# High weights times both token halves in one product of 512 columns, in the mixers and the first fills

## Chip, cores and metric
One core of one Trainium2 chip runs the whole program in one launch. The metric is the time on the device in microseconds, as the median of several executions. TensorE (PE) multiplies, ScalarE (ACT) and VectorE (DVE) copy, split and add, GpSimd (POOL) and the DMA queues of SyncE (SP) bring data.

## What is computed
The reference runs 256 tokens of width 1024 in float32 through two blocks. The first block:

```python
h = rmsnorm(x, norm1_g); proj = h @ w_in
(x_rnn, g_rnn, dq, dk, dv, fq, fk, fv, f_logit, gates) = split(proj)
y_rnn = gelu(g_rnn) * rg_lru(causal_dwconv(x_rnn))
y_diff = rmsnorm(diff_attention(dq, dk, dv))        # 4 heads
y_fox = forgetting_attention(fq, fk, fv, log_f)     # 8 heads
g = sigmoid(gates + gate_b)
x = x + (g[0]*(y_rnn @ w_br_rnn) + g[1]*(y_diff @ w_br_diff) + g[2]*(y_fox @ w_br_fox)) @ w_out
x = x + (gelu(u_gate) * u_val) @ ffn_down           # u = conv(rmsnorm(x) @ ffn_up)
```

The second block has two layers. Each layer is a mixer and an expert stage:

```python
qa, ka, va, qw, kw, vw, gates = split(rmsnorm(h) @ w_in)
oa = dilated_mixture(qa, ka, va); ob = banded_attention(qw, kw, vw)
h = h + (g[0] * (oa @ w_branch_a) + g[1] * (ob @ w_branch_b)) @ w_out
h = h + expert_choice_ffn(rmsnorm(h))               # 16 experts, each on 32 tokens
```

## The kernel before
**Split products.** All dense products but those of the experts are made from split numbers. The normed tokens lie transposed as a high and a low half (`HT.h`, `HT.l`, eight tiles of 128 x 256 each). Weights come in slabs of 128 x 4096 (2 MB) and each slab is cut into four pieces of 128 x 1024. ScalarE copies a piece rounded to its high part (`high`, L1906) and VectorE subtracts this from the piece to get the low part (`low`, L1227). TensorE then adds three products for each tile (`mm3`, L590 to L592): high weights times high tokens, high weights times low tokens, low weights times high tokens. The fourth is left out.

**Pieces and banks.** In the form used for keys, queries and gates (`piece`, with the views `PAIRS`) a piece holds four of the eight row blocks for 256 output columns. Two pieces fill one bank of 128 x 512, with the 128 columns of one group in its left half and those of the next in its right half. So two pieces are 48 products of 256 columns, and ScalarE copies the finished bank out once (`QF`, `KF`, `QW`, `KW`, `QA`, `KA`), or applies tanh with a bias twice (`GT`, `GL`, the gates).

**Buffers for split pieces.** `buffer_plan` gives each piece a buffer and says at which piece of the list the next ones are split (`split_at`). In the first fills (pieces `fq`, `fk` and `gates`, 32 of them) and in the fills of each layer there are three buffers: `split(t)` splits piece t+2, whose buffer was that of piece t-1. In the query and key stage of a layer (`qka`) there are six buffers and `split(t)` splits piece t+5.

**Order of work.** Each engine runs one list in order. Where attention is computed, the order is made by `schedule`: one step is `ffstfwv` in the first fills and `swftfv` in a layer. f is one fill, that is a piece of a later product; s computes scores on TensorE, takes row maxima on VectorE and exponentials on ScalarE; w scales by the row sums on VectorE; t turns tiles on TensorE and copies them on ScalarE or VectorE; v multiplies by the values on TensorE, and ScalarE and VectorE take the output apart into high and low. A step handles s of one unit and w, t and v of the three units before. The first fills have 8 units (4 of one attention, 4 of the other) and 32 fills, the layers 12 units (4 and 8) and 28 fills, two of which are token products of their own kind that the change doesn't touch (`tok_fill`). PE takes `sched_f` and `sched_l` without w; ACT without w and with s as exponentials (`first_exp` L2099, `layer_exp` L2198); DVE with row maxima (L1472).

**Names.** `first_fill` and `layer_fill` exist in the lists of TensorE and ScalarE. `bank_f` and `bank_l` give the bank of each fill. `sides`, `side`, `block`, `query_bank` and `filled` come with the change.

## Time and profile before

| | us |
|---|---|
| median of 3 runs | 1816.87 (1815.5 to 1817.04) |
| the profiled execution, whole | 1819.09 |
| its span, first to last instruction | 1817.3 |
| TensorE busy | 1528.7 (84%) |
| VectorE busy | 762.0 (42%) |
| ScalarE busy | 596.6 (33%) |
| data moved by DMA | 567.44 MB, 312 GB/s on average |

The first block ends near 495 us. The mixer of the first layer runs from there to about 725 us and its experts to 1150 us; the second layer's mixer to about 1385 us and its experts to the end. Busy time tells how much an engine did, the chain of waits what the end waited for, and the timeline in what order an engine took its work. The idle time in brackets in a timeline row stands before that row's first instruction, with the instruction that ended it.

### The profile page before, as it was taken

What the parts mean: (1) busy time and instruction counts of PE and PEld (TensorE: products, weight loads), DVE (VectorE), ACT (ScalarE), POOL (GpSimd) and SP (SyncE); (2) the same over time, 40 slices, a digit from 0 to 9 for tenths busy, and PEclk for the clock granted to TensorE, in tenths of its full rate; (3) what the DMA queues carried; (4) which work ended last, traced back from release to release, by engine and by line L of the source; (5) the groups of instructions that cost most, each with busy time, mean ns of one, the idle gap of its engine ahead of it and who ended that gap; (6) DMA issues with size and microseconds to landing.
All of it is one profiled execution on the core that took longest, in us unless ns stands there. A gap on an engine that the chain in (4) does not pass through costs nothing.

```text
span 1817.3 us, 34044 instructions
## 1 busy us (share of the span) xinstructions
PE 1528.7 (84%) x15288; PEld 1178.5 (65%) x15288; DVE 762.0 (42%) x1574; ACT 596.6 (33%) x1063; POOL 76.0 (4%) x87
## 2 busy tenths in 40 slices
PE   8999999999999999976666656999999966666665
PEld 8989998999799998532333322799896523232332
DVE  6896668887565656210101110546664201011011
ACT  5765546665455654000000000546642000000001
POOL 1020001000020101000000000001010000000000
PEclk9999999999999999997888898999999988888888
DMA  6543446555473568999999999853589999999997
GB/s 263 186 143 140 165 172 235 189 184 200 163 282 120 206 259 352 421 429 430 431 430 429 431 429 430 359 190 129 212 325 412 428 430 430 430 430 429 430 430 310
DMA packets 45841, 567.44 MB, mean 312 GB/s; under 512 B 6672, under 2 KB 7216, under 8 KB 10496
## 3 DMA queue, kind: packets, MB, share of 16 engines
q1 hardware_dynamic: 40176, 552.62, 74.2%
q0 software_dynamic: 3744, 12.03, 1.9%
q8 instruction: 120, 1.97, 0.4%
q10 hardware_dynamic: 1776, 0.62, 0.2%
q14 instruction: 25, 0.20, 0.0%
HBM read 564.18 MB, written 1.05 MB: 311 GB/s over the span
## 4 chain that ended last, share of the span: by engine, by line
PE 60%; DMA 33%; DVE 3%; another core or an unknown queue 2%; ACT 1%; issue 0%; SPq 0%; DVEq 0%; ACTq 0%
DMA slab<-in_slabs 32%; PE bank L590 14%; PE bank L591 14%; PE bank L592 14%; PE bank L1135 6%; PE bank L1187 3%; PE bank L1205 1%; PE bank L947 1%; PE bank L1006 1%; PE bank L970 1%; DMA sm<-in_fb 1%; DVE wl L1227 1%; PE bank L1112 1%; DVE xc L1350 0%
## 5 line engine op out<-in xcount | busy, mean ns | idle before, releaser
L1135 PE MATMUL bank<-slab,xe 128*32 128x256 f32 x4096 | 302.4, 449 | 166.6 <-DMA slab<-in_slabs 166.5
L1227 DVE TENSOR_TENSOR wl<-slab,wh 128x1024 fp32r<-128x1024 f32 (+1 forms) x286 | 348.1, 1231 | 186.4 <-ACT wh L1906 186.1
L590 PE MATMUL bank<-hth,wh 128*128 128x256 f32 x1344 | 387.3, 288 | 1.8 <-DVE wl L1227 1.7
L591 PE MATMUL bank<-htl,wh 128*128 128x256 f32 x1344 | 380.0, 283 | 0.0
L592 PE MATMUL bank<-hth,wl 128*128 128x256 f32 x1344 | 379.9, 283 | 0.0
L1906 ACT ACTIVATE wh<-slab 128x1024 fp32r<-128x1024 f32 (+1 forms) x286 | 296.2, 1046 | 168.9 <-PE bank L592 157.8
L1135 PEld LDWEIGHTS bank<-slab,xe 128*32 128x32 f32 x4096 | 139.5, 125 | 310.1 <-DMA slab<-in_slabs 207.8
L590 PEld LDWEIGHTS bank<-hth,wh 128*128 128x128 f32 x1344 | 257.3, 191 | 11.9 <-issue 7.8
L591 PEld LDWEIGHTS bank<-htl,wh 128*128 128x128 f32 x1344 | 257.5, 192 | 0.1
L592 PEld LDWEIGHTS bank<-hth,wl 128*128 128x128 f32 x1344 | 257.3, 191 | 0.0
L1187 PE MATMUL bank<-slab,ha 128*32 128x256 f32 x2048 | 140.1, 421 | 78.7 <-DMA slab<-in_slabs 77.7
L2302 ACT ACTIVATE ta<-bank 128x256 f32<-128x256 f32 x32 | 12.3, 384 | 516.4 <-PE bank L1135 516.4
L1187 PEld LDWEIGHTS bank<-slab,ha 128*32 128x32 f32 x2048 | 70.6, 118 | 134.0 <-DMA slab<-in_slabs 93.9
L1862 DVE SCALAR_TENSOR_TENSOR ta<-ta,bank 128x256 f32<-128x256 f32 x32 | 13.5, 422 | 287.3 <-ACT ta L2302 287.3
L2308 ACT ACTIVATE ha<-bank 128x256 f32<-128x256 f32 x32 | 12.3, 384 | 273.6 <-PE bank L1170 273.6
L1867 DVE SCALAR_TENSOR_TENSOR ta<-bank,ta 128x256 f32<-128x256 f32 x32 | 13.6, 425 | 209.1 <-PE bank L1135 209.1
L1874 DVE COPY ye<-bank 128x256 f32<-128x256 f32 x32 | 13.6, 425 | 207.9 <-PE bank L1187 207.9
L1205 PE MATMUL bank<-ye,gz 32*128 32x256 f32 x512 | 49.0, 454 | 18.5 <-DVE ye L1874 15.7
L2198 ACT ACTIVATE sx<-sx,sm 128x256 f32<-128x256 f32 (+1 forms) x80 | 41.5, 520 | 60.0 <-DVE sm L1715 43.7
L2386 POOL DMA_DIRECT2D bias<-in_bias x40 | 22.1, 556 | 844.8 <-PE bank L1205 421.1
L1205 PEld LDWEIGHTS bank<-ye,gz 32*128 32x128 f32 x512 | 21.6, 198 | 52.1 <-DVE ye L1874 33.6
L1645 DVE SCALAR_TENSOR_TENSOR u<-bank,pv,u 128x255 f32<-128x255 f32 x88 | 40.4, 480 | 16.5 <-ACT u L2172 14.9
(388 smaller groups left out, 2181.7 us busy)
## 6 DMA issues: line engine op xcount, KB each, us to landing
slab<-in_slabs SPq DMA_DIRECT2D x251, 2048.0 KB, 47.8
slab<-in_slabs SPq DMA_DIRECT2D x23, 1024.0 KB, 10.3
bias<-in_bias POOLq DMA_DIRECT2D x32, 192.0 KB, 3.1
bias<-in_bias POOLq DMA_DIRECT2D x8, 256.0 KB, 5.9
x<-in_x SPq DMA_DIRECT2D x2, 512.0 KB, 4.5
rg<-in_rg POOLq DMA_DIRECT2D x1, 1024.0 KB, 10.4
bt<-in_rel POOLq DMA_DIRECT2D x1, 768.0 KB, 14.6
fg<-in_final_g POOLq DMA_DIRECT2D x1, 512.0 KB, 3.6
```

The source lines that it names most:

```text
L590: e.matmul(o, wh, xh, start=start, stop=False, skip_group_check=True)
L591: e.matmul(o, wh, xl, start=False, stop=False, skip_group_check=True)
L592: return e.matmul(o, wl, xh, start=False, stop=stop, skip_group_check=True)
L947: t = e.matmul(bk[d][:, qb * 256:(qb + 1) * 256], QW[hd, c, qb * 128:(qb + 1) * 128], KW[hd, c // 4, :], start=True, stop=True)
L1135: t = e.matmul(bk[bank][32 * j:32 * j + 32, 0:256], XE[:, c, :], w[:, k, 256 * j:256 * j + 256], start=(c == 0), stop=(c == 7))
L1187: t = e.matmul(bk[3][32 * j:32 * j + 32, 0:256], HA[:, o_:o_ + 32], w[:, k, 256 * j:256 * j + 256], start=(kk == 0), stop=(kk == 7))
L1205: t = e.matmul(bk[b][:, (j % 2) * 256:(j % 2) * 256 + 256], GZ[rows_, tb * 128:(tb + 1) * 128], YE[rows_, :], start=False, stop=(ex == 15) ...
L1227: e.tensor_tensor(lo, src, hi.bitcast(F32), ALU.subtract).then_inc(*dve_l.mark(p))
L1645: t = e.scalar_tensor_tensor(o[:, d:256], ps[:, 0:256 - d], par("fw", (2 - d) * 44 + m), o[:, d:256], ALU.mult, ALU.add)
L1906: e.activation(hi, src, ACT.Copy).then_inc(*act_h.mark(p))
L2198: t = e.activation(S_[:, q * w:(q + 1) * w], S_[:, q * w:(q + 1) * w], ACT.Exp, bias=c_nm[:, st + q:st + q + 1], accum_out=c_dn[:, st + q: ...
L2386: e.dma_start(btiles[n % 4][:, 0:w], I["bias"][n, :, 0:w]).then_inc(*s_bt[n % 4].mark((l, n), 16))
```

## The change
Where it applies, a piece now holds all eight row blocks for 128 output columns (`v_block`, `BLOCKS`). `HT`'s high and low halves are seen as one tile (`HT.both`), so that one product of 512 columns multiplies the high weights by both; the low weights times the high tokens go into the left half of the bank in a second product of 256 columns. The bank then holds two sides of the same 128 x 256 result. ScalarE copies the right side out to the destination (`side`), VectorE adds the left side to it (`sides`), and for gates ScalarE applies tanh to the destination in place, after the add. It applies to all 32 first fills, to 10 of the 12 pieces of each layer's query and key stage, and to 26 of the 28 fills of each layer. The fills alternate between banks 3 and 7. Who waits for `fk`, `qka` or `fill` before scores now waits for VectorE's add.

```diff
+def v_block(c):
+    return lambda ap: ap.rearrange("p (k n) -> p k n", k=8)[:, :, 128 * c:128 * c + 128]
+BLOCKS = [v_block(c) for c in range(4)]
-    add("fq", 0, PAIRS)
-    add("fk", 0, PAIRS)
+    add("fq", 0, BLOCKS)
+    add("fk", 0, BLOCKS)
...
+                self.both = row(name + "b", hi, 2 * n * cols, F32R).rearrange("p (s n c) -> p s n c", s=2, n=n)
+                self.h, self.l = self.both[:, 0, :, :], self.both[:, 1, :, :]
...
+    bank_f, bank_l = {k: 3 if k % 2 else 7 for k in range(32)}, fill_banks(sched_l, 0, 0)
+    bank_l.update({k: 3 if k % 2 else 7 for k in range(4, 28)})
+    bank_l.update({0: 6, 1: 7, 2: 3, 3: 6})
...
+        def block(p, b, X2):
+            wh, wl = halves(p, 8, 128)
+            bank_free(b)
+            for k in range(8):
+                e.matmul(two(bk[b][:, :]), wh[:, k, :], X2.both[:, :, k, :], start=(k == 0), stop=False, skip_group_check=True)
+                t = e.matmul(bk[b][:, 0:256], wl[:, k, :], X2.h[:, k, :], start=False, stop=(k == 7), skip_group_check=True)
+            t.then_inc(*pe_w.mark(p))
...
         def first_fill(k):
             p, b = fills_f[k][0], bank_f[k]
-            piece(p, b, k % 2, 2, 4, HT)
-            if k % 2:
-                reader[b] = [(act_s, ("fk", k // 2 - 2) if 4 <= k < 8 else ("fill", "f", k))]
+            block(p, b, HT)
+            reader[b] = [(dve_s, ("fa", "f", k))]
...
+        def sides(o, b, step):
+            V.wait_ge(*act_s["side", step])
+            e.tensor_tensor(o, o, bk[b][:, 0:256], ALU.add).then_inc(*dve_s.mark(step))
...
         for kind, i in sched_f:
             if kind == "f":
+                V.wait_ge(*pe_w[fills_f[i][0]])
+                dst = QF[:, i, :] if i < 4 else KF[:, i - 4, :] if i < 8 else GT[:, i - 8, :]
+                sides(dst, bank_f[i], ("fa", "f", i))
                 split(fills_f[i][0])
...
+                if 2 <= i < 12:
+                    V.wait_ge(*pe_w[p])
+                    sides((QA if i < 6 else KA)[:, i % 6, :], query_bank(l, i), ("qka", l, i))
                 split(p)
...
-                    for p in fills_l(l)[i]:
+                    ps = fills_l(l)[i]
+                    if len(ps) == 1:
+                        V.wait_ge(*pe_w[ps[0]])
+                        sides(filled(i), bank_l[i], ("fa", l, i))
+                    for p in ps:
                         split(p)
...
+        def side(o, p, b, step):
+            A.wait_ge(*pe_w[p])
+            e.activation(o, bk[b][:, 256:512], ACT.Copy).then_inc(*act_s.mark(("side", step)))
...
         def first_fill(k):
+            dst = QF[:, k, :] if k < 4 else KF[:, k - 4, :] if k < 8 else GT[:, k - 8, :]
+            side(dst, fills_f[k][0], bank_f[k], ("fa", "f", k))
             split(fills_f[k][0])
...
+            n = k - 8
+            if n >= 0:
                 A.wait_ge(*dve_s["hb"])
...
+                A.wait_ge(*dve_s["fa", "f", k])
+                e.activation(GT[:, n, :], GT[:, n, :], ACT.Tanh, bias=c_hb[:, 16 + n:17 + n],
+                             scale=0.5).then_inc(*act_s.mark(("fill", "f", k)))
...
             ps, b = fills_l(l)[k], bank_l[k]
+            if len(ps) == 1:
+                side(filled(k), ps[0], b, ("fa", l, k))
             for p in ps:
                 split(p)
...
+            n = k - 12
+            if n >= 0:
+                A.wait_ge(*dve_s["fa", l, k])
+                e.activation(GL[:, n, :], GL[:, n, :], ACT.Tanh, bias=c_hg[:, 16 * l + n:16 * l + n + 1],
+                             scale=0.5).then_inc(*act_s.mark(("fill", l, k)))
```

## Rows read from the trace of the kernel before

**Rows 1.** The page, chain that ended last, shares of the span
```profile
PE 60%; DMA 33%; DVE 3%; another core or an unknown queue 2%; ACT 1%; issue 0%; SPq 0%; DVEq 0%; ACTq 0%
```

**Rows 2.** Windows: busy us (instructions) of each engine, granted clock, DMA share, GB/s
```profile
630.00:640.00 10.00, 10.00 (x83) 8.95 (x82) 6.89 (x20) 7.24 (x19) 0.00 (x0) 1.00 0.00 0
700.00:710.00 10.00, 10.00 (x46) 8.29 (x45) 5.56 (x6) 3.94 (x4) 0.00 (x0) 1.00 1.01 430
```

**Rows 3.** Timeline of TensorE (start, us, instruction): ends of two unbroken runs
```profile
95.83 0.39 PE L591 MATMUL bank<-wl,hth 128*128 128x512 f32 x1
...
103.99 0.39 PE L591 MATMUL bank<-wl,hth 128*128 128x512 f32 x1
...
153.51 0.28 PE L590 MATMUL bank<-hth,wh 128*128 128x256 f32 x1
...
155.90 0.28 PE L592 MATMUL bank<-hth,wl 128*128 128x256 f32 x1
```

**Rows 4.** Timeline of two steps of the first fills
```profile
148.94 0.28 PE L590 MATMUL bank<-hth,wh 128*128 128x256 f32 x1
...
149.14 0.84 ACT L2128 ACTIVATE gt<-bank,sm 128x256 f32<-128x256 f32 x2 [1.02 <-PE bank L592]
...
152.88 0.29 DVE L1472 CUSTOM_DVE_ANT_0 sd<-bank,bt 128x128 f32<-128x128 f32 x1 [0.60 <-PE bank L796]
...
154.32 0.40 ACT L2099 ACTIVATE sd<-sd,sm 128x128 f32<-128x128 f32 x1 [3.39 <-DVE sm L1541]
...
156.09 1.04 ACT L1906 ACTIVATE wh<-slab 128x1024 fp32r<-128x1024 f32 x1
...
157.17 1.23 DVE L1227 TENSOR_TENSOR wl<-slab,wh 128x1024 fp32r<-128x1024 f32 x1 [2.42 <-ACT wh L1906]
157.75 0.36 ACT L2107 ACTIVATE o<-bank 128x256 f32<-128x256 f32 x1
158.02 1.05 ACT L1906 ACTIVATE wh<-slab 128x1024 fp32r<-128x1024 f32 x1
158.31 0.17 DVE L1547 RECIPROCAL sm<-sm 128x4 f32<-128x4 f32 x1
```

**Rows 5.** Layer 0, one step: chain (TensorE's scores), then timeline of VectorE and ScalarE
```profile
623.44 1.06 PE bank L947 x8
...
632.32 1.06 PE bank L947 x8
...
624.55 0.42 DVE L1472 CUSTOM_DVE_ANT_0 sx<-bank,bias 128x256 f32<-128x256 f32 x1 [0.22 <-PE bank L947]
...
626.44 0.51 ACT L2198 ACTIVATE sx<-sx,sm 128x256 f32<-128x256 f32 x1 [2.58 <-DVE sm L1715]
...
628.52 1.04 ACT L1906 ACTIVATE wh<-slab 128x1024 fp32r<-128x1024 f32 x1
629.47 1.05 ACT L2209 ACTIVATE ptl<-bank 128x512 f32<-128x512 f32 x2
630.43 1.04 ACT L1906 ACTIVATE wh<-slab 128x1024 fp32r<-128x1024 f32 x1
631.38 0.81 ACT L2234 ACTIVATE gl<-bank,sm 128x256 f32<-128x256 f32 x2
...
632.79 0.42 DVE L1745 TENSOR_TENSOR obl<-bank,obh 128x256 fp32r<-128x256 f32 x1
```

**Rows 6.** Chain in order of time: scores of steps 0, 5 and 7, first fills
```profile
122.60 0.86 PE bank L796 x8
...
173.90 1.51 PE bank L811 x16
...
196.79 1.53 PE bank L811 x16
```

**Rows 7.** Timeline of TensorE behind a wait
```profile
34.29 0.39 PE L590 MATMUL bank<-hth,wh 128*128 128x256 f32 x1 [1.67 <-DVE wl L1227]
34.52 0.28 PE L591 MATMUL bank<-htl,wh 128*128 128x256 f32 x1
```

More of the change, by code:

```diff
@@ L163, in piece_list @@
     add("fv", 0, TOKS)
-    add("fq", 0, PAIRS)
-    add("fk", 0, PAIRS)
+    add("fq", 0, BLOCKS)
+    add("fk", 0, BLOCKS)
     for i in range(6):
-        add("gates", i, PAIRS)
+        add("gates", i, BLOCKS)
     for i in range(2):
@@ L180, in piece_list @@
         for i in range(3):
-            add(f"qka{l}", i, PAIRS)
+            add(f"qka{l}", i, BLOCKS if i else PAIRS[0:2] + BLOCKS[2:4])
         add(f"va{l}", 0, TOKS)
         add(f"vb{l}", 0, [v_flat(j, 4, 256) for j in range(2)])
-        add(f"kvw{l}", 0, PAIRS)
+        add(f"kvw{l}", 0, BLOCKS[0:2] + PAIRS[2:4])
         for i in range(2):
-            add(f"qw{l}", i, PAIRS)
+            add(f"qw{l}", i, BLOCKS)
         for i in range(4):
-            add(f"gate{l}", i, PAIRS)
+            add(f"gate{l}", i, BLOCKS)
         add(f"bra{l}", 0, [v_rows(pr, 2) for pr in range(4)])
@@ L801, in fox_scores @@
             c = i - 4
-            for j in range(4):
-                P.wait_ge(*s_l["rows", j])
-            P.wait_ge(*act_s["fk", 1])
+            P.wait_ge(*s_l["rows", 3])
+            P.wait_ge(*dve_s["fa", "f", 7])
             bank_free(0)
@@ L917, in dil_scores @@
             to = dil_parts(qb)
-            P.wait_ge(*act_s["qka", l, 5])
+            P.wait_ge(*act_s["qka", l, 0])
+            P.wait_ge(*dve_s["qka", l, 11])
             for b in range(2):
@@ L938, in win_scores @@
             c = i - 4
-            P.wait_ge(*act_s["fill", l, 2])
-            P.wait_ge(*act_s["fill", l, 5 + c // 2 * 2])
+            P.wait_ge(*dve_s["fa", l, 2])
+            P.wait_ge(*dve_s["fa", l, 4 + c])
             for b in range(2):
@@ L1017, in layer_fill @@
                 return
-            j = k - 1 if k < 3 else k % 2
-            piece(ps[0], b, j, 2, 4, HT)
-            if j:
-                reader[b] = [(act_s, ("fill", l, k))]
+            block(ps[0], b, HT)
+            reader[b] = [(dve_s, ("fa", l, k))]
             if k == 27:
@@ L1027, in tensor_program @@
             norm(f"m{l}")
-            for n in range(6):
-                b = rot["qka", l, n]
-                pair(first[f"qka{l}", 0] + 2 * n, b, 2, 4, HT, None if n else f"m{l}")
-                reader[b] = [(act_s, ("qka", l, n))]
+            pair(first[f"qka{l}", 0], rot["qka", l, 0], 2, 4, HT, f"m{l}")
+            reader[rot["qka", l, 0]] = [(act_s, ("qka", l, 0))]
+            for i in range(2, 12):
+                b = query_bank(l, i)
+                block(first[f"qka{l}", 0] + i, b, HT)
+                reader[b] = [(dve_s, ("qka", l, i))]
             banks = (rot["va", l, 0], rot["va", l, 1])
@@ L1758, in vector_program @@
             for p in range(first[f"qka{l}", 0], first[f"vb{l}", 0]):
+                i = p - first[f"qka{l}", 0]
+                if 2 <= i < 12:
+                    V.wait_ge(*pe_w[p])
+                    sides((QA if i < 6 else KA)[:, i % 6, :], query_bank(l, i), ("qka", l, i))
                 split(p)
@@ L2225, in layer_fill @@
                 return
-            if k == 1 or k >= 4 and k % 2 == 0:
-                return
-            A.wait_ge(*pe_w[ps[0]])
-            if k < 12:
-                dst = KW if k == 2 else QW[:, k - 5:k - 3, :]
-                t = e.activation(dst, two(bk[b][:, :]), ACT.Copy)
-            else:
-                for n in (k - 13, k - 12):
-                    t = e.activation(GL[:, n, :], bk[b][:, (n % 2) * 256:(n % 2 + 1) * 256], ACT.Tanh,
-                                     bias=c_hg[:, 16 * l + n:16 * l + n + 1], scale=0.5)
-            t.then_inc(*act_s.mark(("fill", l, k)))
+            n = k - 12
[3 more added lines that the diff above has]
+                             scale=0.5).then_inc(*act_s.mark(("fill", l, k)))
         for l in range(2):
@@ L2247, in scalar_program @@
             for n in range(6):
-                p, b = first[f"qka{l}", 0] + 2 * n, rot["qka", l, n]
+                p = first[f"qka{l}", 0] + 2 * n
+                if n:
+                    side((QA if n < 3 else KA)[:, 2 * n % 6, :], p, query_bank(l, 2 * n), ("qka", l, 2 * n))
                 split(p)
+                if n:
+                    side((QA if n < 3 else KA)[:, 2 * n % 6 + 1, :], p + 1, query_bank(l, 2 * n + 1), ("qka", l, 2 * n + 1))
                 split(p + 1)
-                A.wait_ge(*pe_w[p + 1])
-                dst = QA if n < 3 else KA
-                e.activation(dst[:, 2 * n % 6:2 * n % 6 + 2, :], two(bk[b][:, :]), ACT.Copy).then_inc(*act_s.mark(("qka", l, n)))
+                if n == 0:
+                    A.wait_ge(*pe_w[p + 1])
+                    e.activation(QA[:, 0:2, :], two(bk[rot["qka", l, 0]][:, :]), ACT.Copy).then_inc(*act_s.mark(("qka", l, 0)))
                 if n == 1:
```

22 lines of the change are left out of this document (7 added, 15 removed).

## The prediction
> **What bounds the kernel now.** I read the chain of waits first, then TensorE's own state in the stages that the diff touches, then the timeline of one step of each loop. The chain is 60% TensorE and 33% slab DMA [rows 1]: the reader sees that two resources take turns. Which of them holds in the changed stages is seen in the windows: at 630 to 640 us, in the middle of the first layer's attention, TensorE is busy for all 10.00 us and the slab DMA for none, while at 700 to 710 us, after the mixer, DMA runs at share 1.01 and 430 GB/s [rows 2]. So a microsecond that TensorE gains or loses in the first fills or in a mixer moves the start of the saturated DMA stretch behind it by a microsecond, since every slot that opens there is opened by TensorE's progress; I pass changes on in full, both times. The other thing to see is that TensorE waits for nobody in these loops today. The question is only whether ScalarE and VectorE, which now get more to do between two products, still keep up.
>
> **Part 1, the products.** One 256-column product every 0.1195 us: 20 steps from 153.51 to 155.90. One 512-column product every 0.2267 us: 36 steps from 95.83 to 103.99 [rows 3]. Both runs are unbroken. Two of the short ones cost 0.239, one long one 0.2267, so joining two saves 0.0123 to 0.0132 us (the second with the rounder 0.12 spacing); I take 0.0132. A group of 128 output columns costs 24 short products today, 2.88 us, and 8 long plus 8 short after, 2.77 us: 8 joins, 0.106 us saved. There are 32 such groups in the first fills, and in each of two layers 10 in the query and key stage and 26 among the fills: 104 groups, 11.0 us. Nothing here alternates 512 and 256 columns, so I bound a group between 2.72 us (the fixed part gone from the short ones) and 2.88 us (nothing saved), and take 2.77, between the two unbroken runs.
> The Trainium skill (TensorE: Matmul & The Clock Gate, Back-to-back issue gap) gives a lone product's spacing as columns over 2.4 GHz plus about 2.5 ns. By it a join would save 2.5 ns and the whole change 2 us instead of 11; the same section gives 131 ns for 512 columns in a stream, by which it would be far more. The trace has 226.7 ns, so it agrees with neither: the part that doesn't grow with the columns is 13 ns here.
>
> **Part 2, where the work of the fills moves.** Read the order of waits in the code, not the busy shares. In the fills there are three buffers for split weights, so the split made at piece p is that of piece p+2, and it needs the buffer of piece p-1. Before, ScalarE at fill p waited only for the end of p-1; VectorE's low part followed. After, both engines first wait for the end of piece p itself (to take its two sides out) and only then make p+2. The weights of p+2 are thus started a whole group later, with one group of 2.77 us and whatever attention work lies between as cover. The path behind the end of a group is: visible to ScalarE 0.20 after TensorE's slot ends (148.94 to 149.14), copy of one side 0.27 to 0.30 until the next instruction starts (157.75 to 158.02, the nearest row: 256 columns from a bank), the high part 1.04 and the low part behind it at 1.08 after the high's start (156.09 to 157.17), the low part 1.14 until VectorE's next start [rows 4]. That is 0.20 + 0.30 + 1.08 + 1.14 = 2.72 until VectorE is free, 2.8 until the product can start: bare fills would just hold. VectorE's add (a 256-column one from a bank, 0.42 by [rows 5]) lies beside ScalarE's high part and costs nothing there. What doesn't hold is the attention work queued behind it on both engines.
>
> **First fills (32 groups), the loop.** A step is two fills, scores s(i), a turn t, a third fill, weights w, values v. VectorE's row maximum for s(i) now stands behind the low part that is made after the second fill. Chain from the end of that fill: 2.72 to VectorE free (before, the maximum was taken as soon as the scores stood, with no low part to wait for); maximum and its negation 1.44 until ScalarE starts the exponentials (152.88 to 154.32); these 1.77 (154.32 to 156.09); then the side of the third fill 0.30, its high part 1.08, its low part 1.23, and 0.05 to the product: 8.6 us [rows 4]. Then the group itself, 2.77, whose end is the next step's start: 11.4 us a step. Today five steps take 51.30 us (122.60 to 173.90), 10.26 each, which the cheaper groups would make 9.94, and the next two 22.89 [rows 6]. After: 57.0 for the five, +5.7; the next two, of which the later heads' ScalarE copy of a turned tile lengthens one by about 0.4, 23.15, +0.3. Ahead of them two groups, -0.2. Behind them nine groups (-1.0) with one wait that I estimate at 2.1 us, since the head norm's VectorE instructions stand in the same queue: +1.1. Together **+6.9 us**.
>
> **Layers, 26 groups among the fills, twice.** One step today: 8.88 us (623.44 to 632.32); with two cheaper groups TensorE needs 8.67. The loop through the other two engines: maximum to exponentials 1.89 (624.55 to 626.44), exponentials 2.08 (to 628.52), side 0.30, high part 0.95 (to 629.47), tanh from the copied tile 0.36, two turned tiles 0.96 (to 630.43), side 0.30, high part 1.05, 0.05 to VectorE, low part 1.14, the low part of the output 0.35: 9.4 us [rows 5]. Today the same loop is without the two sides and the tanh between, 8.5 us, and the tanh pair of 0.81 (631.38) is hidden beside a low part; that is why TensorE never waits now though it is close. After, the loop wins by 0.77 us a step in the steps with gate fills. Pieces made ahead cover the first of the six such steps and most of the second, about 4.6 less 1.6, and behind the last scores, where TensorE's step is 1.06 shorter but the exponentials still run, one wait is 1.8: some 4.8 us of waits against 26 x 0.106 = 2.8 saved. **+2.0 us a layer, +4.0**.
> **Query and key stage, 10 groups, twice.** Six buffers: the weights made at p are used five pieces on, some 11 us after the end of p. ScalarE spends 0.30 + 0.95 and VectorE 0.35 + 1.14 on a group of 2.77 us, with no attention in the queue, and four banks turn: hidden, so **-2.1 us**. If this cover went, it would be the 2.8 us path against 2.77, that is nothing.
> **Restarts.** After a wait for VectorE the second product comes 0.23 after the first instead of 0.12 (34.29 to 34.52) [rows 7]. Some ten waits stand where no attention product already pays that: +1.1 us.
> **Tanh from a tile, bank use, DMAs.** The gates' tanh waits for VectorE's add; on ScalarE the turned tile, the next side and the next high part are queued behind it, as counted. The banks alternate and a fill's bank is free after its add, one group before it is wanted. Slabs are given back one group later, 3 us in a stage whose DMA has whole idle windows [rows 2]: nothing.
> **Sum.** 6.9 + 4.0 - 2.1 + 1.1 = +9.9 us. The profiled run took 1819.09 us (span 1817.3 and 1.8 around it), so 1829.0 in its terms; the median lies 2.2 below it: **1826.8 us**.
>
> **Rivals.**
> A, faster: the cover holds. The two engines' later start is absorbed and TensorE never waits; then the 11.0 us stand: 1805.9. It decides from the point where the loop of the first fills is under 9.94 instead of 11.4 and that of the layers under 8.67 instead of 9.4. For it: bare fills just hold and ScalarE is busy for only 7.24 of 10 us [rows 2]. Against: the busy share counts no order, and the chain above has no slack in it. Chance 0.06.
> B, no change: only the first fills lose (+6.9 and 1.0), the layers' loop is under 8.67, for instance because side and add are shorter than the rows for them: 6.9 + 1.0 - 5.5 - 2.1 = +0.3, 1817.2. Chance 0.13.
> C, a join saves nothing (or the moving operand in two runs of 256 columns is slower): a group is 2.88. The loops grow by 0.11 where a group is in them, and all that ran uncovered loses its gain; with the same chains the first fills lose 1.6 more, a layer 1.1 more, and the query and key stage gains nothing: 8.5 + 2 x 3.1 + 0 + 1.1 = +15.8: 1832.7. For it: no row has this alternation. Chance 0.14. The skill's 2.5 ns would lead nearly here.
> D, the clock. The granted clock is 1.00, the 2.4 GHz level, through both windows of [rows 2], and stayed there over the 1.67 us wait of [rows 7] (the spacing behind it is 0.12). If the waits of 1 to 2 us in each step brought TensorE to the 1.2 GHz level for a tenth of the 115 us of first fills, it would lose about another 12 us: 1838. Chance 0.05. The Trainium skill (TensorE: Matmul & The Clock Gate, A second HAM failure mode: psum-queue depth-cycling) tells of short idles between groups that make the clock swing; the trace speaks against it for a single wait, and no row shows a train of them.
>
> **How the numbers follow.** Forecast 0.60 (1820 to 1832 by itself: copies of 0.2 to 0.5 us and groups of 2.72 to 2.88 give +5 to +15), A 0.06, B 0.13, C 0.14, D 0.05, others 0.02. The range reaches down to B and up through C: 1816.5 to 1835. A measurement tells 0.2%, 3.6 us, from no change. Slower by more: the forecast but for 0.01, C and D, 0.79; within: B, 0.13 and 0.01 of the forecast's low edge; faster: A and 0.01 of the others, 0.07 (the other 0.01 goes with slower).
>
> **What would show it.** The long products every 0.227 us and the short every 0.12, groups of 2.77; steps of the first fills 11.4 us apart, all alike; layer steps growing to 9.4; TensorE waiting some 10 us in the first fills and 5 in each layer, each time for VectorE's low part; query and key stage waiting for nothing. If TensorE's idle time in the fills is under 5 us in all, my reading of the order is wrong; if steps are alike but shorter, the side or the add is cheaper than its row; if a group is 2.88, the join is worth nothing.

## The result, and the profile after

The median of the changed kernel is 1829.03 us (1826.8 to 1831.72, 4 runs) against 1816.95 us (1815.5 to 1817.04, 4 runs) of the kernel before on the same chip: ratio 1.0069, 95% interval 1.0057 to 1.0081. It is slower by 12.1 us; the prediction said slower by 9.9 and 1826.8. The profiled execution took 1828.15 us (span 1826.4), 9.1 more than that of before. It lies only 9.1 and not 12.1 higher mainly because its first product of the values (`dv`) happened to start 2.72 us earlier, at 92.18 instead of 94.90, ahead of everything that the change touches (in the ten profiles of this case that start lies between 91.93 and 96.98). From that product to the end the two traces differ by 11.8 us.

The page of after: busy times, the chain by engine, and the three groups of the changed pieces (the two products, and VectorE's low part).

```profile
PE 1547.3 (85%) x14456; PEld 1139.6 (62%) x14456; DVE 800.7 (44%) x1678; ACT 615.3 (34%) x1143; POOL 76.4 (4%) x87
...
PE 46%; DMA 33%; DVE 10%; ACT 8%; another core or an unknown queue 2%; issue 1%; DVEq 0%; SPq 0%; ACTq 0%
...
L1253 DVE TENSOR_TENSOR wl<-slab,wh 128x1024 fp32r<-128x1024 f32 (+1 forms) x286 | 348.4, 1230 | 110.4 <-ACT wh L1947 110.0
...
L652 PE MATMUL bank<-htb,wh 128*128 128x512 f32 x832 | 304.8, 407 | 14.0 <-DVE wl L1253 9.9
L653 PE MATMUL bank<-htb,wl 128*128 128x256 f32 x832 | 234.0, 281 | 0.0
```

In [rows 1] the chain was 60% TensorE and 4% VectorE and ScalarE together. Now it is 46% TensorE and 18% the two others: the chain runs through them where before it ran straight along TensorE. The DMA share is the same 33%. All of TensorE's idle time in the changed pieces stands before the first long product of a group (L652), none before a short one.

The windows that answer [rows 2] (columns as there): one at the last scores of the first layer's attention, one behind the attention, where the DMA is saturated.

```profile
640.00:650.00 10.00, 9.46 (x61) 7.49 (x61) 7.12 (x22) 7.27 (x20) 0.00 (x0) 1.00 0.01 2
708.00:718.00 10.00, 10.00 (x46) 8.27 (x45) 5.82 (x6) 3.68 (x4) 0.00 (x0) 1.00 1.00 427
```

TensorE was busy for 10.00 of 10 us in the attention before and is now for 9.46. ScalarE is busy for 7.27 us, as good as before (7.24), and VectorE for 7.12 instead of 6.89. ScalarE and VectorE are far from full, and yet TensorE waits and the stage is longer. Behind it the DMA runs at 1.00 and 427 GB/s as before.

The times of the same products in both traces say where the 11.8 us arise (starts in us; a stage is the difference of two rows):

| start of | before | after | stage: after less before |
|---|---|---|---|
| first product of `dv` | 94.90 | 92.18 | (outside the change) |
| first scores of the first fills | 122.53 | 125.25 | +5.44 |
| scores of step 7 | 196.72 | 202.39 | +2.95 |
| first product behind the first fills | 230.33 | 237.31 | +1.31 |
| norm of layer 0 | 495.64 | 502.61 | -0.01 |
| first scores of layer 0 (query and key stage between) | 544.23 | 550.67 | -0.53 |
| router of layer 0 | 718.20 | 726.46 | +1.82 |
| norm of layer 1 (experts, DMA) | 1153.61 | 1161.39 | -0.48 |
| first scores of layer 1 | 1203.87 | 1211.12 | -0.53 |
| router of layer 1 | 1377.84 | 1386.89 | +1.80 |
| end | 1817.3 | 1826.4 | +0.05 |

What stands between the changed stages passes the loss on, as the prediction took it. From the end of the first fills to the norm of layer 0 it is TensorE's own work (busy for 98.85 of 100 us from 300 to 400 us, DMA share 0.57) and changes by -0.01 us. The two experts' stages, where the DMA share is 1.01 and 0.98, change by -0.48 and +0.05.

**The loop of the first fills.** The chain of waits in order of time, one step of it (start, us, what). It answers the chain that [rows 6] had, where these steps were TensorE's alone.

```profile
148.87 1.87 ACT sd L2144 x8
150.74 0.27 ACT gt L1956
151.00 0.96 ACT wh L1947
151.98 1.24 DVE wl L1253
153.26 0.50 PE bank L652
...
156.19 0.13 PE bank L653
156.34 0.38 ACT gt L1956
156.73 0.95 ACT wh L1947
157.71 1.23 DVE wl L1253
158.93 0.20 DVE sd L1502
...
160.08 0.18 DVE sm L1571
160.28 1.87 ACT sd L2144 x8
```

The loop of the prediction can be read link by link: exponentials, side out, high part, low part, one group of products, side, high part, low part, row maximum, and the exponentials again 11.41 us later. The exponentials head the chain at 148.87, 160.28, 171.74, 183.19, 194.61 and 206.44: 11.41, 11.46, 11.45, 11.42 and 11.83 us apart. The prediction's sum, cut at the same places:

| link | predicted | measured |
|---|---|---|
| exponentials to the side | 1.77 | 1.87 |
| side to the high part | 0.30 | 0.26 |
| high part to the low part | 1.08 | 0.98 |
| low part to the product | 1.28 | 1.28 |
| group, to the next side | 2.97 | 3.08 |
| side to the high part | 0.30 | 0.39 |
| high part to the low part | 1.08 | 0.98 |
| low part to the row maximum | 1.14 | 1.22 |
| row maximum to the exponentials | 1.44 | 1.35 |
| step | 11.36 | 11.41 |

No link is off by more than 0.11 us. What the loop costs depends on what TensorE needs for the same step, and before the change that was not 10.26 us each time. The steps of the first fills, from scores to scores (us):

| | 0 to 1 | 1 to 2 | 2 to 3 | 3 to 4 | 4 to 5 | 5 to 6 | 6 to 7 |
|---|---|---|---|---|---|---|---|
| before | 9.73 | 9.68 | 9.97 | 10.63 | 11.29 | 11.28 | 11.61 |
| after | 9.79 | 9.78 | 11.42 | 11.46 | 11.45 | 11.41 | 11.83 |

Of the +2.95 us, 2.28 are lost in two steps, 2 to 3 and 3 to 4. From step 4 on TensorE's own work takes nearly as long as the loop, which costs only 0.13 to 0.22 us a step there.

Where TensorE waits, by releaser (us in total, times, longest), first for 100 to 250 us, then for 580 to 700:

```profile
PE bank L652 <- DVE wl L1253: 4.1, 4, 1.8
PE bank L652 <- ACT vf L2021: 3.8, 1, 3.8
...
PE bank L652 <- DVE wl L1253: 2.9, 4, 1.6
```

The first and the third line are what was expected in kind: VectorE's low part ends the wait, four times in each stage. The sizes are less than half of what was expected in the first fills (4.1 us for some 10) and little more than half in a layer (2.9 for 5). The second was not expected.

**The first wait of the fills.** Timeline of after at the start of the first fills (start, us, instruction, idle time before it and its releaser), TensorE, ScalarE and VectorE, and the window around it:

```profile
118.58 1.04 ACT L1947 ACTIVATE wh<-slab 128x1024 fp32r<-128x1024 f32 x1
119.53 1.06 ACT L2021 ACTIVATE vf<-bank 128x512 f32<-128x512 f32 x2
...
120.73 0.47 PE L652 MATMUL bank<-htb,wh 128*128 128x512 f32 x1 [3.80 <-ACT vf L2021]
...
122.11 0.63 PE L652 MATMUL bank<-htb,wh 128*128 128x512 f32 x1
...
122.54 1.96 DVE L1555 SCALAR_TENSOR_TENSOR bt<-bt,cmask 128x384 f32<-128x384 f32 x4
...
124.41 0.41 DVE L1262 TENSOR_TENSOR qf<-qf,bank 128x256 f32<-128x256 f32 x1
...
125.25 0.93 PE L823 MATMUL bank<-kd,qd 64*128 64x128 f32 x8
```

```profile
120.00:130.00 10.00, 9.27 (x46) 7.63 (x47) 8.80 (x20) 5.13 (x10) 0.00 (x0) 0.83 0.59 216
```

Fill 1 goes into bank 3, and bank 3 still holds the values, which ScalarE takes out (`vf`) only at 119.53, behind a high part that itself stands behind the recurrence. Before, the first two fills shared bank 7 and bank 3 was wanted one fill later; the trace of before has the same copy at the time of the first scores (122.53), and no wait of TensorE for it:

```profile
122.26 1.06 ACT L1976 ACTIVATE vf<-bank 128x512 f32<-128x512 f32 x2
```

Now TensorE stands for 3.80 us. From 0.8 us behind that wait the products go at the 1.2 GHz level: the long one at 122.11 is followed by the next at 122.75, 0.64 us later instead of 0.35, and the granted clock of the window is 0.83 where [rows 2] had 1.00. Fill 1 takes 4.52 us from its first product to the scores, where a group takes 2.83; so the wait of 3.80 and the clock's 1.7, less 0.1 for two cheaper groups, make the stage's +5.44.

**The layer's loop.** Timeline of after, layer 0, one step (answering [rows 5]):

```profile
638.14 1.14 PE L973 MATMUL bank<-kw,qw 64*128 64x256 f32 x8
...
639.81 0.50 PE L652 MATMUL bank<-htb,wh 128*128 128x512 f32 x1 [0.53 <-DVE wl L1253]
...
642.58 0.41 DVE L1502 CUSTOM_DVE_ANT_0 sx<-bank,bias 128x256 f32<-128x256 f32 x1
...
644.47 0.51 ACT L2238 ACTIVATE sx<-sx,sm 128x256 f32<-128x256 f32 x1 [2.73 <-DVE sm L1748]
...
646.55 0.36 ACT L1956 ACTIVATE gl<-bank 128x256 f32<-128x256 f32 x1
646.82 1.04 ACT L1947 ACTIVATE wh<-slab 128x1024 fp32r<-128x1024 f32 x1
...
647.50 1.13 PE L973 MATMUL bank<-kw,qw 64*128 64x256 f32 x8
```

From one step's scores to the next it is 9.36 us here, with 8.88 before and 9.4 predicted. Maximum to exponentials is 1.89 (642.58 to 644.47), the exponentials 2.08 (to 646.55), the side 0.27: the rows of before, carried over. But of the eleven steps between scores this is the last and the only one of that length. The three before it take 8.75, 8.75 and 9.07 us, where those of before take 8.88 or 8.89. TensorE's four waits are 0.24, 0.53, 0.54 and 1.61 us long, the last two behind the last scores, and the second layer's are the same within 0.02 us.

**The products.** Timeline of after in the query and key stage, where nothing waits (answering [rows 3]):

```profile
523.87 0.40 PE L652 MATMUL bank<-htb,wh 128*128 128x512 f32 x1
524.11 0.28 PE L653 MATMUL bank<-htb,wl 128*128 128x256 f32 x1
...
525.29 0.40 PE L652 MATMUL bank<-htb,wh 128*128 128x512 f32 x1
525.52 0.28 PE L653 MATMUL bank<-htb,wl 128*128 128x256 f32 x1
```

Four pairs take 1.42 us, and over the whole stage a pair takes 0.353, where the two unbroken runs of [rows 3] would make 0.346. A group of eight pairs is 2.83 us, not 2.77: the join saves 0.052 us a group, half of what was taken.

### The profile page after: what moved, and what is told of

Same layout as the page of the kernel before. It is cut to its first block, busy times and chain, and to the rows that moved or that the text cites. A ratio compares the mean times of both kernels' runs of the same rounds, so it can differ in the third digit from the quotient of the medians.

```text
span 1826.4 us, 32687 instructions
## 1 busy us (share of the span) xinstructions
PE 1547.3 (85%) x14456; PEld 1139.6 (62%) x14456; DVE 800.7 (44%) x1678; ACT 615.3 (34%) x1143; POOL 76.4 (4%) x87
## 3 DMA queue, kind: packets, MB, share of 16 engines
q8 instruction: 114, 1.87, 0.4%
HBM read 564.18 MB, written 1.05 MB: 309 GB/s over the span
## 4 chain that ended last, share of the span: by engine, by line
PE 46%; DMA 33%; DVE 10%; ACT 8%; another core or an unknown queue 2%; issue 1%; DVEq 0%; SPq 0%; ACTq 0%
DMA slab<-in_slabs 32%; PE bank L608 7%; PE bank L610 7%; PE bank L609 7%; PE bank L652 6%; PE bank L1161 6%; DVE wl L1253 3%; PE bank L653 3%; ACT wh L1947 3%; PE bank L1213 3%; ACT sx L2238 2%; DVE sx L1502 1%; PE bank L1231 1%; PE bank L1138 1%
## 5 line engine op out<-in xcount | busy, mean ns | idle before, releaser
L1161 PE MATMUL bank<-slab,xe 128*32 128x256 f32 x4096 | 312.9, 461 | 149.3 <-DMA slab<-in_slabs 149.3
L1161 PEld LDWEIGHTS bank<-slab,xe 128*32 128x32 f32 x4096 | 143.2, 127 | 300.2 <-DMA slab<-in_slabs 191.4
L652 PE MATMUL bank<-htb,wh 128*128 128x512 f32 x832 | 304.8, 407 | 14.0 <-DVE wl L1253 9.9
L653 PE MATMUL bank<-htb,wl 128*128 128x256 f32 x832 | 234.0, 281 | 0.0
L1213 PE MATMUL bank<-slab,ha 128*32 128x256 f32 x2048 | 144.0, 431 | 73.9 <-DMA slab<-in_slabs 73.1
L652 PEld LDWEIGHTS bank<-htb,wh 128*128 128x128 f32 x832 | 157.0, 189 | 60.4 <-DVE wl L1253 20.7
L653 PEld LDWEIGHTS bank<-htb,wl 128*128 128x128 f32 x832 | 158.1, 190 | 0.0
L608 PE MATMUL bank<-htb,wh 128*128 128x256 f32 x512 | 145.8, 285 | 0.0
L609 PE MATMUL bank<-htb,wh 128*128 128x256 f32 x512 | 144.9, 283 | 0.0
L610 PE MATMUL bank<-htb,wl 128*128 128x256 f32 x512 | 144.9, 283 | 0.0
L608 PEld LDWEIGHTS bank<-htb,wh 128*128 128x128 f32 x512 | 98.2, 192 | 0.9 <-DVE wl L1253 0.4
L609 PEld LDWEIGHTS bank<-htb,wh 128*128 128x128 f32 x512 | 98.3, 192 | 0.1
L610 PEld LDWEIGHTS bank<-htb,wl 128*128 128x128 f32 x512 | 98.3, 192 | 0.0
L1231 PE MATMUL bank<-ye,gz 32*128 32x256 f32 x512 | 53.5, 492 | 18.6 <-DVE ye L1915 15.8
```

The costliest lines, as they stand in the source:

```text
L608: e.matmul(o, wh, xh, start=start, stop=False, skip_group_check=True)
L609: e.matmul(o, wh, xl, start=False, stop=False, skip_group_check=True)
L610: return e.matmul(o, wl, xh, start=False, stop=stop, skip_group_check=True)
L652: e.matmul(two(bk[b][:, :]), wh[:, k, :], X2.both[:, :, k, :], start=(k == 0), stop=False, skip_group_check=True)
L653: t = e.matmul(bk[b][:, 0:256], wl[:, k, :], X2.h[:, k, :], start=False, stop=(k == 7), skip_group_check=True)
L1161: t = e.matmul(bk[bank][32 * j:32 * j + 32, 0:256], XE[:, c, :], w[:, k, 256 * j:256 * j + 256], start=(c == 0), stop=(c == 7))
```

## The experiments

The theory to test: the change loses by its order. Both engines take the sides of piece p out before they split piece p+2, so the split stands behind a group's end, and attention work stands behind the split. The first rival: it is the products themselves (the joined product saves nothing, or its alternation with the short one costs). The second: it is the amount of added work, the copy and the add on ScalarE and VectorE, wherever they stand.

### bank5: fill 1 into a bank that is free

```diff
+    bank_f[1] = 5
```

> The second first fill writes bank 5 instead of bank 3, which is still waiting for ScalarE's copy of fv. Theory (the loop over ScalarE and VectorE sets the pace of the first fills): TensorE's 3.8 us wait for that copy and the stretch of low clock behind it go, 5.4 us, but the loop has its 11.4 us steps from the first one on, so only about 3 us of it come back: 1826. Rival (waits add up, the early one is simply extra): all of 5.4 comes back, 1823.6. Rival (the copy was not what held it): nothing, 1829.

Measured: 1829.95 us (1827.89 to 1831.47), ratio 1.007 (1.0057 to 1.0082) against 1816.94. No gain: a miss. TensorE's waits from 100 to 250 us:

```profile
PE bank L653 <- DVE qf L1263: 4.4, 1, 4.4
PE bank L653 <- DVE wl L1254: 4.2, 4, 1.8
```

The wait for `vf` is gone, and a longer one stands in its place, for VectorE's add of fill 0 (`qf`), which frees bank 7 for fill 2. In the timeline of after above, that add runs at 124.41, behind two low parts, the recurrence's last gate and the relative bias (122.54, 1.96 us). The first scores come 16.69 us before the second (119.66 and 136.35) instead of 9.8; the next step is 9.84 and after that they are 11.4 again. So two things are late at this place, and the bank was only the first: the start is set by what is queued on VectorE as well. From 0.7 us before the end of the wait of 4.4 us the granted clock is at half, for 6.8 us.

### grouped: eight long products, then eight short ones

```diff
             for k in range(8):
                 e.matmul(two(bk[b][:, :]), wh[:, k, :], X2.both[:, :, k, :], start=(k == 0), stop=False, skip_group_check=True)
+            for k in range(8):
                 t = e.matmul(bk[b][:, 0:256], wl[:, k, :], X2.h[:, k, :], start=False, stop=(k == 7), skip_group_check=True)
```

> All eight long products of a group first, then its eight short ones. Theory (alternating 512 and 256 columns costs 3 or 4 ns a product over unbroken runs): a group takes 2.77 us instead of 2.83; the query and key stages gain 1.1 us, the loops, in which a group stands once per step, some 2 more: 1826. Rival (the pace comes from something else, such as where the operands lie): pairs stay at 0.353 on average and the time at 1829.

Measured: 1829.47 us (1827.12 to 1829.83), ratio 1.0065 (1.0053 to 1.0077). The pace came out: a group is 2.793 us instead of 2.827, long products every 0.230 and short ones every 0.120, so the alternation does cost some 0.034 us a group. The time did not. 0.034 us on 104 groups is 3.5 us at the most, and in the loops only one group of a step counts. In its profile the first fills run at half the granted clock for 6.8 us around the wait for `vf` and for 3.4 us near 218 us, where after has 3.4 us in all, and from `dv` to the end of the first fills it took 147.39 us against 145.13. So what the grouping gives is smaller than what these spells take in this one profile. Where no spell disturbs, its gain can be read: the two query and key stages are 0.34 us shorter each than in after, and the two layers' attention with its fills, from first scores to router, 0.16 and 0.13, some 1.0 us in all.

### three_short: the order of the change with the products of before

```diff
             for k in range(8):
-                e.matmul(two(bk[b][:, :]), wh[:, k, :], X2.both[:, :, k, :], start=(k == 0), stop=False, skip_group_check=True)
+                e.matmul(bk[b][:, 0:256], wh[:, k, :], X2.h[:, k, :], start=(k == 0), stop=False, skip_group_check=True)
+                e.matmul(bk[b][:, 256:512], wh[:, k, :], X2.l[:, k, :], start=False, stop=False, skip_group_check=True)
                 t = e.matmul(bk[b][:, 0:256], wl[:, k, :], X2.h[:, k, :], start=False, stop=(k == 7), skip_group_check=True)
```

> The joined product is taken apart: high weights times high tokens to the left half, high weights times low tokens to the right half, low weights times high tokens to the left half, 24 products of 256 columns; all copies, adds, orders and banks stay. Theory: a group takes 2.88 us instead of 2.83, and the loops lengthen by that: about 3 us more, 1832. Rival (the join is the cause of the slowdown, the new order is harmless): back at 1817.

Measured: 1831.35 us (1829.53 to 1836.78), ratio 1.0085 (1.0071 to 1.01). Timeline of TensorE in the query and key stage:

```profile
523.80 0.28 PE L652 MATMUL bank<-htb,wh 128*128 128x256 f32 x1
523.92 0.28 PE L653 MATMUL bank<-htb,wh 128*128 128x256 f32 x1
524.04 0.28 PE L654 MATMUL bank<-htb,wl 128*128 128x256 f32 x1
```

Every 0.12 us, 2.88 a group, exactly the products of before. With no joined product at all the kernel still loses 14 us. The first rival falls, and the loss is made elsewhere. The join is worth 2.3 us to the good by the medians, whose intervals overlap, and 3.1 us by the traces: 0.8 in the first fills, 0.5 in each query and key stage, 0.6 in each layer's attention.

### layers_only: the change in the two layers, the first fills as before

```diff
-    add("fq", 0, BLOCKS)
-    add("fk", 0, BLOCKS)
+    add("fq", 0, PAIRS)
+    add("fk", 0, PAIRS)
...
-        add("gates", i, BLOCKS)
+        add("gates", i, PAIRS)
...
-    bank_f, bank_l = {k: 3 if k % 2 else 7 for k in range(32)}, fill_banks(sched_l, 0, 0)
+    bank_f, bank_l = fill_banks(sched_f, 0, 2), fill_banks(sched_l, 0, 0)
```

with `first_fill` on TensorE and ScalarE, VectorE's part of it and the waits ahead of the later heads' scores as before.

> The changed kernel with its first fills as before (half pieces, one ScalarE copy for two groups); the layers have the change. Theory: the first fills carry most of the loss, so 1820 to 1822. Rival (the layers carry it): 1826 or more.

Measured: 1820.61 us (1817.17 to 1823.05), ratio 1.002 (1.0011 to 1.0029) against 1816.72. TensorE's waits in layer 0 (540 to 700 us):

```profile
PE bank L652 <- DVE wl L1255: 2.9, 4, 1.6
```

The same four waits and the same 2.9 us as in the whole change. By the medians 3.9 of the 12.1 us are the layers' and 8.2 the first fills', but the interval of the 3.9 reaches from 2.0 to 5.3. The stages of the traces divide it more sharply: with its first fills as before (135.42 us from `dv` to their end, 135.43 before), layers_only loses 1.79 us from the first scores to the router in each layer and gains 0.54 in each query and key stage, 2.5 us together; the first fills of after lose 9.7.

### early_late_tanh: splits ahead of the sides

Both engines make the split of piece p+2 first and wait for the end of piece p only then; so that the gates' tanh does not wait in ScalarE's queue for an add that now stands behind a low part, it is done one fill later. In the first fills on VectorE (the layers, and ScalarE, alike):

```diff
-                V.wait_ge(*pe_w[fills_f[i][0]])
                 dst = QF[:, i, :] if i < 4 else KF[:, i - 4, :] if i < 8 else GT[:, i - 8, :]
-                sides(dst, bank_f[i], ("fa", "f", i))
                 split(fills_f[i][0])
+                V.wait_ge(*pe_w[fills_f[i][0]])
+                sides(dst, bank_f[i], ("fa", "f", i))
...
-            n = k - 8
-            if n >= 0:
+            for m in [k - 1] + [31] * (k == 31):
+                n = m - 8
+                if n >= 0:
```

> In the fills ScalarE makes the high part and VectorE the low part of the piece after next before they wait for the current group, as they did before the change, and ScalarE takes the tanh of a gate one fill later. Same instructions, other order. Theory (order, not load): in the first fills TensorE's waits for low parts nearly vanish, in the layers about 3 us of waits stay, now for VectorE's add of the group before; some 9 us less than the changed kernel, 1820. Rival (load: the added copies and adds are too much for the two engines or slow TensorE by contention): the same work in any order costs the same, 1828 to 1830.

Measured: 1823.67 us (1822.19 to 1826.18), ratio 1.0038 (1.0027 to 1.0049). TensorE's waits, 100 to 250 us and then 580 to 700:

```profile
PE bank L652 <- ACT vf L2021: 3.8, 1, 3.8
PE bank L652 <- DVE gt L1262: 1.0, 1, 1.0
...
PE bank L652 <- DVE gl L1262: 2.7, 3, 1.7
```

Nothing waits for a low part any more. Scores of step 0 to scores of step 7 took 73.83 us, against 77.14 in after and 74.19 before: the loop of the first fills is open, and with the cheaper groups a little under its old time. The result is 5.4 us better than after, with every instruction of it still there. It stays above the 1820 that was expected. What is left of the loss shows in its trace: the start of the fills is no better (33.95 us from `dv` to the first scores, 33.07 in after, 27.63 before), and in the layers, as expected, the wait has only changed hands: the bank is now freed by an add (`gl`) that stands behind a low part.

### early_only: the same without the late tanh

```diff
-            for m in [k - 1] + [31] * (k == 31):
-                n = m - 8
-                if n >= 0:
+            n = k - 8
+            if n >= 0:
```

> As early_late_tanh, but the tanh stays in its own fill, so on ScalarE the next high part is queued behind a tanh that waits for VectorE's add, which is itself queued behind a low part. Theory (order): worked out with the same durations, this order closes a longer loop over ScalarE and VectorE in the gate steps, about 10.3 us a step in the layers against 8.8; some 35 us over early_late_tanh: 1850 to 1862. Rival (the gain of early_late_tanh came from the earlier splits alone, where a tanh stands doesn't matter): 1824.

Measured: 1858.91 us (1856.68 to 1859.7), ratio 1.023 (1.0216 to 1.0244): 35 us slower than its neighbour, by the place of one instruction. Waits of TensorE, 100 to 250 us and then 540 to 700:

```profile
PE bank L652 <- DVE sm L1577: 4.9, 7, 1.3
...
PE bank L652 <- DVE gt L1262: 2.9, 2, 1.8
...
PE bank L652 <- DVE gl L1262: 11.6, 7, 2.8
```

ScalarE's tanh waits for VectorE's add, the add for VectorE's low part before it, the low part for ScalarE's high part: a round trip in each fill, and the exponentials stand behind it. The last three steps of layer 0 take 10.9, 13.1 and 10.7 us, where 10.3 had been worked out.

### high_ahead: the high part ahead of the exponentials

early_late_tanh, and ScalarE makes the next fill's high part before it waits for the row maximum, in the time that it idled there (2.2 to 2.6 us in a step of the first fills' loop in after, 2.73 in a layer's).

```diff
             elif kind == "s":
+                n = next(k for what, k in sched_f[at_:] if what == "f")
+                split(fills_f[n][0])
+                ahead.add(("f", n))
                 first_exp(i)
```

and the same ahead of `layer_exp`.

> As early_late_tanh, and ScalarE makes the high part of the next fill before the exponentials, in the time in which it only waited for VectorE's row maxima (2.6 us before each). Banks and products as in the changed kernel. Theory (order): the loop of the layers falls under TensorE's own 8.76 us a step and the layers gain 1.3 us each instead of losing 1.8; the first fills keep the loss of their start, for the bank of the second fill and VectorE's late arrival: 1816. Rival (load): 1824 as before the move.

Measured: 1816.35 us (1814.81 to 1819.21), ratio 1.0 (0.9992 to 1.0009). Waits of TensorE among the fills, from 100 to 250 us, all of them (from 540 to 700 there is none):

```profile
PE bank L652 <- ACT vf L2021: 3.8, 1, 3.8
```

The layer's last four steps are 8.75 us each (8.88 or 8.89 before, up to 9.36 in after). All of the loss is back with nothing removed: the same copies, adds and tanhs as in the changed kernel. This is the run that speaks most plainly against the second rival, the amount of work. The balance is a sum of two parts: from `dv` to the end of the first fills it is still 138.74 us, 3.3 more than before, for the start is as late as in after (33.07), and the layers make up for that, with 1.44 us less than before from first scores to router and 0.5 less in the query and key stage, twice.

### all_ahead: and the start of the fills

high_ahead with the grouped products, the first fills in banks 7, 5, 3, 6 instead of 7, 3, 7, 3, and VectorE's relative bias not before the first maximum needs it.

```diff
+    bank_f.update({1: 5, 2: 3, 3: 6})
...
             elif kind == "s":
+                if i == 0:
+                    relative_bias()
                 first_max(i)
```

> high_ahead, and the first four first fills take banks 7, 5, 3, 6 so that none waits for a copy; VectorE prepares the relative bias only before the first maxima; a group's eight long products run before its eight short ones (2.79 us instead of 2.83). Theory: TensorE waits almost nowhere and nearly all of the saved 0.087 us times 104 shows: 1808. Rival (a wait or half-clock stretch elsewhere takes it): 1814 or more.

Measured: 1808.76 us (1807.85 to 1808.97), ratio 0.9955 (0.9941 to 0.9969) against 1816.72, faster than the kernel before by 8.0 us and than the changed one by 20. Of TensorE's waits from 95 to 700 us these belong to fills:

```profile
PE bank L653 <- DVE qf L1264: 1.6, 1, 1.6
...
PE bank L653 <- ACT vf L2026: 0.2, 1, 0.2
```

The wait of 3.8 us at the start, and the 4.4 that bank5 put in its place, have become 0.2 and 1.6, and no half clock shows before 780 us. From `dv` to the end of the first fills it takes 134.32 us (145.13 after, 135.43 before). Three edits were added to high_ahead at once. From `dv` to the end of the first fills, where all three act, its trace is 4.4 us shorter than high_ahead's; in the query and key stages and the layers' attention, where only the grouping acts, 1.3 us together. What each of the three gives in the first fills was not measured.

## Why the prediction was right, and where it was only right in sum

**Right: the mechanism.** The splits moved behind a group's end, and the chain through ScalarE and VectorE became longer than TensorE's own work. The first-fills loop was put at 11.4 us and is 11.41 to 11.46; the layer's at 9.4 and is 9.36 where it holds, in the last step between scores. Each wait in the loops ends with VectorE's low part, and the query and key stage waits for nothing, as said. Taking the splits out of that place again (early_late_tanh, high_ahead) gives 5.4 and 12.7 us back, with the added work left in; taking the join away (three_short) gives nothing back. Rival A (the cover holds) and B (only the first fills lose) are out: both stages lost. The traces put the loss of the two layers' fills at 1.82 and 1.80, where +2.0 each and a share of the restarts had been summed.

**Mis-sized: the group, in part 1.** 2.77 was taken between 2.72 and 2.88; it is 2.83 in most groups. Grouping the products measures 2.793, so a half of the gap lies in the alternation and the rest in the long product's 0.230 against 0.2267. So the 104 groups save 5.4 us and not 11.0, and the query and key stages 0.53 us each and not 1.05. Rival C (a group of 2.88) was wrong too: three_short has these 2.88 and is 2.3 us slower by the medians.

**Failed: "a fill's bank is free after its add, one group before it is wanted: nothing".** True from fill to fill, and not for the first one: bank 3's reader before fill 1 is ScalarE's copy of the values. The prediction read the new map of banks only against itself. The row of it in the kernel before was there to be read: this copy ran at 122.26, with the first scores of the fills at 122.53. The step cost +5.44 where the ahead groups had been put at -0.2. bank5 shows that the map alone does not mend it, for VectorE comes as late with the first add.

**Failed the other way: five steps of 11.4 from the first scores on.** The first two steps are 9.79 and 9.78 (125.25, 135.04, 144.82), and only then 11.42. Six buffers turn ahead of the fills, so when the first scores begin at 125.25 the weights up to fill 4 are split and those of fills 5 and 6 come next: in the trace of after VectorE makes the low parts of fills 2 to 6 at 118.53, 120.27 (two), 124.74 and 126.72, while TensorE is at fills 1 and 2. That `split(t)` splits piece t+2 holds only from fill 5 on: by `buffer_plan` the splits of fills 0 and 1 make pieces 5 and 6, and those of fills 2 to 4 make none. I counted such pieces for the layers and forgot them here. Two steps at TensorE's pace save 3 us: step 0 to step 7 lost 2.95 us and not 6.0. The average of 10.26 us a step hid that the steps before the change grow from 9.73 to 11.29, which leaves the loop of 11.4 little to cost in the later ones.

**Mis-sized: the cover, in the layers.** The prediction let the pieces made ahead cover the first of six steps with gate fills and most of the second, and summed 4.8 us of waits against 2.8 us saved. The cover holds for three steps (8.57, 8.75 and 8.75 us) and most of the fourth (9.07), and the waits are 2.9 us. The saving is half as well, 26 times 0.053 or 1.4 us. Both terms were too large and stood against each other (2.9 less 1.4 and the restarts make +1.8), so that +1.8 lies near +2.0 is luck. The same holds for the waits as a whole: for low parts there are 9.9 us where some 20 were forecast. The sign of failure that the prediction gave itself, under 5 us of idle time in the fills in all, did not come, but in the first fills it is the wait for `vf` that keeps it away: without it they have 4.1.

**So the sum** has for the first fills +9.7 instead of +6.9 (start +5.4 instead of -0.2, steps +2.95 instead of +6.0, the tail +1.3 as against +1.1), -1.06 instead of -2.1 for the query and key stages, +3.6 for the layers' fills instead of +4.0, both with their restarts, -0.5 in the experts' stage, where DMA took up a little, and nothing beside them for the restarts, whose price was right (the first pair behind a wait takes 0.46 us, 153.26 to 153.72, instead of 0.35) and which these differences hold: 11.8 instead of 9.9. An error of 5.6 us at the start and one of 3 us in the steps stood against each other, with smaller ones behind them: that the total came within some 2 us is in good part luck.

**The clock, rival D.** It was put at a tenth of the first fills and a train of short waits as its cause. In after the train is thin: from 130 to 230 us there are four waits, 1.38, 0.73, 0.19 and 1.78 us long and 11 to 35 us apart, and they left the granted clock at 1.00. early_only has the dense one, a wait of 0.2 to 1.3 us in each step from 142 us on and two of up to 1.8 behind the steps, and its clock stays at 1.00 as well, from 126 to 507 us. The single wait of 3.80 us did not: 3.4 us at half clock follow, 1.7 us lost. The Trainium skill (TensorE: Matmul & The Clock Gate, A second HAM failure mode: psum-queue depth-cycling) has the clock swing with short idles between groups; in this kernel neither train brought that about. All seven profiles with a wait of 3.8 to 4.4 us at the start of the fills (after, bank5, grouped, three_short, early_late_tanh, early_only, high_ahead) have a spell at half clock there, while layers_only and all_ahead, which have no such wait, have none before 780 us. early_only has more of 3.4 us: in each layer two, behind its two longest waits (2.64 to 2.75 us, while those of 2.57 and less there have none), and one at 508 us, in the norm of layer 0, behind waits of 0.77 and 0.97 us that before and after have too, without a spell.

**What stays open.** Which of all_ahead's three edits its 4.4 us in the first fills come from. Whether grouping by itself changes the kernel's time: 1829.47 against 1829.03 cannot be told apart, though the traces show some 1.0 us outside the first fills. And why the profile of grouped has a second spell of half clock near 218 us, behind a wait of 1.80 us, where after has one of 1.78 and no spell.

## What to carry to other kernels

When an edit moves a wait, write down for each in-order engine what stands behind it, and close the loop through all engines link by link from the trace's start-to-start times; here that gave 11.36 for a measured 11.41, while the engines' busy shares showed nothing. Then set the loop against each step's own time, not against an average, and count in the buffer plan how many steps the work made ahead covers. The cure is of the same kind: work that depends on nothing late (a split for a later piece) belongs into the idle stretch ahead of a dependent instruction, and work that waits for another engine belongs one turn later. When buffers or banks are dealt out anew, look up the last reader of each from before the stage, and when that reader's engine gets to it, for the first turn is not the steady one.

## What the hardware showed that was not expected

- A product of 512 columns followed by one of 256 takes 0.353 us as a pair, against 0.2267 and 0.1195 in unbroken runs. In some fills, such as the six pairs from 153.72 to 155.79, it is 0.345. Eight and eight in two blocks take 2.793 us, alternating 2.83.
- A wait of TensorE of 3.8 us came with 3.4 us at half the granted clock in after, three_short and high_ahead, and with 6.8 us in grouped, early_late_tanh and early_only, at the same wait; bank5's 4.4 us came with 6.8. In the three with 3.4 us the clock fell 0.8 to 0.9 us after the wait had ended, in the four with 6.8 us 0.7 to 1.9 us before its end. What decides between the two was not found. The four waits of 0.2 to 1.8 us in the loop of the first fills had no spell with them in after. At half clock a long product comes every 0.427 us and a short one every 0.213, about twice the rest.
- The order of the same instructions on two engines that are busy for some 7 of 10 us each in the attention was worth 42.6 us: 1858.91 (early_only) to 1816.35 (high_ahead).
